# The second MLP's second product as seven products of halves, its operands streamed in steps

## What is computed

```python
def sqrelu_mlp(h, w1, w2):
    a = jax.nn.relu(h @ w1)
    return (a * a) @ w2
...
        x = x + g2 * sqrelu_mlp(hx2, w_mlp1[l], w_mlp2[l])
    return x
```

## Time and profile before

| | us |
|---|---|
| median of 3 executions | 2749.87 |
| lowest, highest | 2747.62, 2750.0 |
| the profiled execution's own time | 2747.8 |
| its span, first to last instruction | 2746.0 |
| TensorE busy in it | 2674.3 |
| the second MLP's first product (2081.2 to 2394.4) | 313.2 |
| the second MLP's second product (2394.4 to 2742.7) | 348.3 |

### The profile page before, as it was taken

The page is one execution under the profiler, slowest core; times in us unless marked ns, Lnnn a source line. Parts: engine busy times, 40 slices in busy tenths (PEclk is TensorE's granted clock), DMA queues, the critical chain, the costliest instruction groups (busy, mean ns, idle before and its releaser), DMA issues.

```text
span 2746.0 us, 41687 instructions
## 1 busy us (share of the span) xinstructions
PE 2674.3 (97%) x17264; PEld 2236.6 (81%) x17264; DVE 1582.8 (58%) x2224; ACT 1074.9 (39%) x1735; POOL 178.9 (7%) x153
## 2 busy tenths in 40 slices
PE   8999999999999999997899999999899999999999
PEld 7887878778888888886889878877787888888887
DVE  6445454476665797866525555566657656654443
ACT  6444454544434322126232443344445555521110
POOL 2222212300000000005100000000000000000000
PEclk9999999999999999999899999999999999999999
DMA  4111111213333786752323221121631333442221
GB/s 134 40 40 32 40 32 33 93 31 119 107 112 116 279 318 222 276 192 77 118 78 122 64 73 48 50 73 48 221 123 37 117 115 101 149 157 94 99 77 69
DMA packets 243676, 297.05 MB, mean 108 GB/s; under 512 B 10528, under 2 KB 190240, under 8 KB 243488
## 3 DMA queue, kind: packets, MB, share of 16 engines
q1 hardware_dynamic: 243488, 294.38, 32.0%
HBM read 238.77 MB, written 55.57 MB: 107 GB/s over the span
## 4 chain that ended last, share of the span: by engine, by line
PE 73%; ACT 4%; DVE 3%; DMA 1%; issue 1%; POOL 0%; SPq 0%; ACTq 0%; DVEq 0%
PE ps L841 8%; PE ps L850 8%; PE ps L844 8%; PE ps L807 7%; PE ps L809 7%; PE ps L811 7%; PE ps L529 2%; PE ps L513 2%; PE ps L1028 2%; PE ps L516 2%; PE ps L1029 2%; PE ps L1033 2%; PE ps L599 2%; PE ps L595 2%; PE ps L597 2%; PE ps L1003 1%
## 5 line engine op out<-in xcount | busy, mean ns | idle before, releaser
L1333 ACT ACTIVATE Whi<-Wraw 128x1024 fp32r<-128x1024 f32 x164 | 171.7, 1056 | 708.0 <-PE ps L850 433.3
L1882 DVE TENSOR_TENSOR Wlo<-Wraw,Whi 128x1024 fp32r<-128x1024 f32 x152 | 189.5, 1253 | 427.3 <-ACT Whi L1333 427.1
L807 PE MATMUL ps<-Bh,Ah 128*128 128x512 f32 x896 | 350.5, 391 | 5.3 <-ACT wb L1511 3.5
L809 PE MATMUL ps<-Bh,Al 128*128 128x512 f32 x896 | 349.2, 390 | 0.0
L841 PE MATMUL ps<-a_h,Whi 128*128 128x512 f32 x1024 | 316.0, 390 | 0.7 <-DVE R L1919 0.7
L844 PE MATMUL ps<-a_h,Wlo 128*128 128x512 f32 x1024 | 315.3, 389 | 0.0
L850 PE MATMUL ps<-a_l,Whi 128*128 128x512 f32 x1024 | 252.9, 389 | 0.0
L811 PE MATMUL ps<-Bl,Ah 128*128 128x512 f32 x640 | 249.0, 389 | 0.0
L595 PE MATMUL ps<-Whi,Hh 128*128 128x256 f32 x768 | 223.5, 291 | 7.6 <-ACT Hh L1364 7.6
L599 PE MATMUL ps<-Whi,Hl 128*128 128x256 f32 x768 | 220.0, 286 | 8.0 <-DVE Hl L1912 8.0
L841 PEld LDWEIGHTS ps<-a_h,Whi 128*128 128x128 f32 x1024 | 192.2, 188 | 41.4 <-DVE R L1919 1.1
(11 more groups left out here) (346 smaller groups left out, 4950.6 us busy)
## 6 DMA issues: line engine op xcount, KB each, us to landing
pair<-in_m_w SPq DMA_DIRECT2D x64, 512.0 KB, 5.4
a_scratch<-ub SPq DMA_DIRECT2D x128, 256.0 KB, 2.0
Wraw<-in_m_w SPq DMA_DIRECT2D x64, 512.0 KB, 4.2
a_r<-a_scratch SPq DMA_DIRECT2D x64, 512.0 KB, 5.3
Wraw<-in_w_in SPq DMA_DIRECT2D x56, 512.0 KB, 4.1
n<-in_w_ada SPq DMA_DIRECT2D x32, 512.0 KB, 5.0
mraw<-in_w_ada SPq DMA_DIRECT2D x32, 512.0 KB, 5.7
R<-in_xT SPq DMA_DIRECT2D x16, 512.0 KB, 4.5
```

The costliest lines, as they stand in the source:

```text
L807: e.matmul(o, h[:, k, :], Bh[x][:, k, :], start=first and k == 0, stop=False, skip_group_check=not first)
L809: e.matmul(o, l[:, k, :], Bh[x][:, k, :], start=False, stop=False, skip_group_check=not first)
L1333: e.activation(Whi[n % 4][:], Wraw[n % 2][:], ACT.Copy).then_inc(*S("w_hi").tick(n))
L1882: e.tensor_tensor(Wlo[n % 4][:], Wraw[n % 2][:], Whi[n % 4][:].bitcast(F), ALU.subtract).then_inc(*S("w_lo", "v").tick(n))
```

## The change

The second product of the second MLP becomes seven products of halves, once over all hidden features. The hidden features are halved (even and odd tiles of 128), the output features are halved (0 to 511 and 512 to 1023), and the tokens are halved. Each of the seven products is 512 outputs by 2048 hidden features by 512 tokens. The products come in the order 1, 5, 6, 2, 7, 3, 4 (`SX`), and each is cut into 8 steps of 256 hidden features, so there are 56 steps g. A step is 4 output tiles by 2 inner tiles by 3 matmuls, 24 matmuls.

- Four of the seven feature operands are sums or differences of quarters. VectorE makes the four of a group in the first product (`feature_sums`), and SP writes seven tiles a group instead of four, to `b_scratch`. The quarters of the second MLP now lie in two sets of seven buffers `qb`, which take `R1`'s place in SBUF. So `R1` is written to `xs_scratch` ahead of the first product and read back during the first 8 of the steps loaded later (`x_load(3, ...)`).
- The weights of products 5, 6, 7 and 3 are sums or differences too. VectorE makes them per step as the operands come (`step_sum`), for 5 and 7 from two loads, for 6 and 3 from one load and what product 5 left.
- Operands have 8 places. A step is loaded into its place when the step 8 before it is done (`step_load`), split by ScalarE and VectorE (`step_split`), and used once.
- Products 1, 6, 7 and 4 go on adding in the same two PSUM tiles, 5, 2 and 3 use the other two. A product's result is added to one or two quarters of `R1` (`add_part`, 4 operations of 128x512 each), eight such parts in all, in place of 64 additions of 128x1024. The last product's final 3 steps go tile by tile.

```diff
-        a_d = nc.dram_tensor("a_scratch", [64, P, T], F, kind="Internal").ap()
+        a_d = nc.dram_tensor("a_scratch", [32, P, T], F, kind="Internal").ap()
+        b_d = nc.dram_tensor("b_scratch", [7, 16, P, 512], F, kind="Internal").ap()
...
+        qb = [[at(f"qb{p}{i}", [P, 512], F, R1A + 14336 * p + 2048 * i) for i in range(7)] for p in range(2)]
+        places = [(S_(4), S_(5), S_(8), S_(9)), (S_(6), S_(7), S_(10), S_(11)), (H_(10), H_(11), H_(2), H_(3)),
...
-        WT += [cols256(m2_w2, 256 * j, 512 * i) for i in range(8) for j in range(4)]
...
+        SX = (1, 5, 6, 2, 7, 3, 4)
+        PART = {1: [(0, 0)], 5: [(0, 1), (1, 1)], 6: [(0, 1)], 2: [(0, 0)], 7: [(1, 1)], 3: [(0, 1)], 4: [(1, 0)]}
+        WGT = {1: [(0, 0)], 5: [(1, 0), (1, 1)], 6: [(0, 0)], 2: [(0, 1)], 7: [(0, 0), (1, 0)], 3: [(0, 1)], 4: [(1, 1)]}
+        FTR = {1: 0, 3: 1, 2: 2, 5: 3, 7: 4, 6: 5, 4: 6}
+        PLACE_LAST = (1, 5, 2, 7, 7, 4, 3, 3)
...
+        def quarter_buf(u):
+            return ub[u % 3] if u < 64 else qb[u // 4 % 2][u % 4]
...
+                if j:
+                    return stream()
...
+            def stream():
+                for i, x in enumerate(SX):
+                    banks = (0, 3) if x in (1, 6, 7, 4) else (1, 2)
+                    if x in (1, 5, 2, 3):
+                        for h, b in enumerate(banks):
+                            PS[stream_bank(x, 2 * h)] = b, filled[b]
+                            empty(b, filled[b])
+                            filled[b] += 1
...
+                    elif x in (6, 7, 4):
+                        pe.wait_ge(*(part_out(SX[i - 2], 0, m) for m in range(4)))
+                    o = lambda m: psum[banks[m // 2]][:, HALF[m % 2]]
+                    cont = x in (6, 7, 4)
+                    def parts(g, m, k):
+                        wh, wl, fh, fl = (t[g % 8] for t in (wgt_h, wgt_l, ftr_h, ftr_l))
+                        ws, fs = slice(512 * k + 128 * m, 512 * k + 128 * m + 128), HALF[k]
+                        return (wh[:, ws], fh[:, fs]), (wh[:, ws], fl[:, fs]), (wl[:, ws], fh[:, fs])
+                    def ready(g, n):
+                        if n == 0:
+                            pe.wait_ge(S("a_hi").at(32 + 2 * g), S("a_hi").at(33 + 2 * g))
+                        else:
+                            pe.wait_ge(S("a_lo").at(31 + 2 * g + n))
+                    together = 5 if x == 4 else 8
+                    for g in range(8 * i, 8 * i + together):
+                        for n in range(3):
+                            ready(g, n)
+                            mk = [(m, k) for m in range(4) for k in range(2)]
+                            for m, k in sorted(mk, key=lambda t: t[1]) if n < 2 else mk:
+                                a, b = parts(g, m, k)[n]
+                                done = n == 2 and k == 1
+                                last = done and g % 8 == 7
+                                ins = e.matmul(o(m), a, b, start=not cont and g == 8 * i and n == 0 and k == 0, stop=last,
+                                               skip_group_check=cont)
...
+                    if together < 8:
+                        for m in range(4):
+                            for g in range(8 * i + together, 8 * i + 8):
...
+            def feature_out(q, i):
+                v = 64 + 7 * (q - 16) + i
+                if v >= 67:
+                    sp.wait_ge(S("a_out", v % 3).at(v - 3))
+                e.dma_start(b_d[i, q - 16], qb[q % 2][3 if i == 4 else 4 if i == 3 else i][:]).then_inc(
+                    *S("a_out", v % 3).tick(v, 16))
+            def sums_out(q):
+                for n in range(4):
+                    sp.wait_ge(S("t_sum").at(4 * q + n))
+                    feature_out(q, 3 + n)
+            def step_load(g):
+                x, kk, p = SX[g // 8], g % 8, g % 8
+                if g >= 8:
+                    sp.wait_ge(stream_full(g - 8))
+                else:
+                    sp.wait_ge(product_full(STEP[PLACE_LAST[g], 31]))
+                    if g == 7:
+                        sp.wait_ge(S("c_scaled").at(127))
+                if g >= 4:
+                    sp.wait_ge(S("a_hi").at(33 + 2 * (g - 4)))
...
+                for n, (mh, kh) in enumerate(WGT[x]):
+                    if n:
+                        if g == 8 or g == 9:
+                            sp.wait_ge(S("a_part_hi").at(STEP[3, 30]), S("a_part_lo").at(STEP[3, 30]))
+                        else:
+                            sp.wait_ge(S("a_sum").at(2 * NS + (g - 2 if kk >= 2 else g - 18)))
+                    e.dma_start(two((other[g % 2] if n else wgt_r[p])), rows[kh][:, 2 * kk:2 * kk + 2, 512 * mh:512 * mh + 512]
+                                ).then_inc(*S("a_raw", g % 4).tick(32 + g, 16))
+                sp.wait_ge(f_out(16 + 2 * kk, FTR[x]), f_out(17 + 2 * kk, FTR[x]))
+                e.dma_start(two(ftr_r[p]), b_d[FTR[x], 2 * kk:2 * kk + 2].rearrange("q p c -> p q c")).then_inc(
+                    *S("a_raw", g % 4).tick(32 + g, 16))
+            def stream_loads():
+                last = 2 * NS
+                quarter_out(last - 3)
+                step_load(3)
+                step_load(4)
+                quarter_out(last - 2)
+                step_load(5)
+                step_load(6)
+                sums_out(31)
+                for g in range(7, 56):
+                    if 8 <= g < 16:
+                        sp.wait_ge(f_out(31, 6), f_out(31, 5), f_out(31, 4))
+                        x_load(3, g - 8, xs_d[g - 8])
+                    step_load(g)
+                    if g in (42, 50):
+                        result_out(2 if g == 42 else 7)
+                result_out(3)
+                result_out(4)
...
+                for m in range(8 * j):
+                    sp.wait_ge(out_at((PROJ[j], m), m // 7))
+                    e.dma_start(xs_d[m], R1[:, m, :]).then_inc(*S("xs_out").tick(1, 16))
                 for s in range(NS * j, NS * j + NS):
                     x, q = SEQ[s]
                     if x == 4 and q % 16 < 14:
                         pair_load(q + 2)
                     if s % NS >= 3:
+                        if SEQ[s - 3][0] == 2 and SEQ[s - 3][1] > 16:
+                            sums_out(SEQ[s - 3][1] - 1)
                         quarter_out(s - 3)
+                    if j:
+                        if s - NS in (107, 108, 111):
+                            step_load((107, 108, 111).index(s - NS))
+                        continue
...
+                if j:
+                    return stream_loads()
...
-                if u >= 3:
+                if q >= 18:
+                    dve.wait_ge(f_out(q - 2, (0, 1, 2, 4)[n]), S("t_sum").at(4 * (q - 2) + 3))
+                elif q >= 16:
+                    dve.wait_ge(S("xs_out").at(1), S("lo", "v").at(b_lo(1, 3, 3)))
+                elif u >= 3:
...
+            def feature_sums(q):
+                b11, b22, b21, b12, t1, t2_, t4 = (t[:] for t in qb[q % 2])
+                dve.wait_ge(S("c_sq").at(4 * q + 3))
+                if q >= 18:
+                    dve.wait_ge(f_out(q - 2, 3), f_out(q - 2, 5), f_out(q - 2, 6))
+                e.tensor_tensor(t1, b12, b11, ALU.subtract).then_inc(*S("t_sum").tick(4 * q))
+                dve.wait_ge(S("t_sum").at(4 * q))
+                e.tensor_tensor(b12, b22, b12, ALU.subtract).then_inc(*S("t_sum").tick(4 * q + 1))
+                e.tensor_tensor(t2_, b22, t1, ALU.subtract).then_inc(*S("t_sum").tick(4 * q + 2))
+                dve.wait_ge(S("t_sum").at(4 * q + 2))
+                e.tensor_tensor(t4, b21, t2_, ALU.subtract).then_inc(*S("t_sum").tick(4 * q + 3))
+            def step_sum(g):
...
+                dve.wait_ge(S("a_raw", g % 4).at(32 + g))
+                if x == 5:
+                    if g == 8:
+                        dve.wait_ge(product_full(2 * NS - 1), S("a_part_lo").at(2 * NS - 1))
+                    i = e.tensor_tensor(wgt_s[kk][:], wgt_r[p][:], other[g % 2][:], ALU.add)
+                elif x == 6:
+                    dve.wait_ge(S("a_hi").at(33 + 2 * (g - 8)), S("a_lo").at(33 + 2 * (g - 8)))
+                    i = e.tensor_tensor(wgt_s[kk][:], wgt_s[kk][:], wgt_r[p][:], ALU.subtract)
+                elif x == 7:
+                    i = e.tensor_tensor(wgt_r[p][:], wgt_r[p][:], other[g % 2][:], ALU.subtract)
+                else:
+                    dve.wait_ge(S("a_sum").at(2 * NS + 16 + kk))
+                    i = e.tensor_tensor(wgt_r[p][:], wgt_r[p][:], wgt_s[kk][:], ALU.subtract)
+                i.then_inc(*S("a_sum").tick(2 * NS + g))
+            def step_split(g):
+                p, x, kk = g % 8, SX[g // 8], g % 8
+                dve.wait_ge(S("a_hi").at(32 + 2 * g))
+                e.tensor_tensor(ftr_l[p][:], ftr_r[p][:], ftr_h[p][:].bitcast(F), ALU.subtract).then_inc(
+                    *S("a_lo").tick(32 + 2 * g))
...
+            def add_part(x, a):
+                mh, hf = PART[x][a]
+                for m in range(4):
```

(29 more changed lines are left out.)

107 lines of the change are left out of this document (83 added, 24 removed).

## The result

The changed kernel takes **2702.94 us** (median of 4 executions, 2702.66 to 2703.14) beside 2748.74 for the kernel before (median of 4, 2747.6 to 2750.0). The ratio is 0.9833, 95% interval 0.9816 to 0.985. The forecast was 2705 in a range of 2700 to 2720.

What follows compares the result with a forecast made beforehand. TensorE, busy 97% of the span, was taken as the bound, the second product being the pure sum of its matmuls. 2747.8 - 43.5 - 0.4 = 2703.9 us, put at 2705 towards the three executions' median; range 2700 to 2720.

Steps and rivals of the forecast that it cites:

- The sum on TensorE: Second product: 1536 matmuls removed, 1344 added at 226.7 ns each, so 43.5 us less and a stage of 304.7 us.
- The boundary: Before the first product's last quarter: TensorE's 1.03 us wait for ScalarE's copy shortens as ScalarE is free sooner, -0.4 us.
- The tail: Kernel end: half a tile's addition and one 256 KB store landing in 2.0 us, as before; 0, bounds -0.5 and +0.5.
- Saving `R1`: Before the second stage: 8 stores of 512 KB, 7 under the projection, the last landing before the first quarter is due; 0.
- The operands of the stream: Second stage's loads: 74 MB, 244 GB/s average, peak 385 in product 5, covered by loading 7 steps ahead; cost 0.
- 27 us stay: Product 5's prefetch: of a 38 us lead, landing up to 7.4 and sum with low parts 3.7 go, 27 remain.
- Rival A: Second stage: operands late at times from slower landing; with two thirds of the lead lost, some 10 us, 2715; chance 0.08.
- VectorE and ScalarE in the stream: Second stage: VectorE works 201 us and ScalarE 119 of 304.7, costing 0 while the cover holds.
- The first product: Four added sums, 2.8 us a group, 44 us in all, hidden by about 4 us of cover and VectorE's waits; 0.
- Rival B: First product: VectorE's sums come out, about 1 us each period without the cover, 16 us in all, 2721; chance 0.05.
- The clock behind a wait: After a 1.86 us TensorE wait the clock fell to 0.50 for some 2.7 us; another 1.4 us lost each time.
- The chances: Forecast with small terms (2700 to 2711) 0.78; range 2700 to 2720 a little over 0.8; faster by over 0.2% 0.94.

Runs made afterwards that it cites:

- e7_mmorder: Changed kernel with all three kinds of matmul of a stream step going tile by tile in one order: 2700.3 us.
- e1_lead4: Changed kernel with a step's loads waiting for the step 4 before it instead of 8: 2705.06 us.
- e2_lead3: Changed kernel with a step's loads waiting for the step 3 before it instead of 8: 2745.24 us.
- the moved sums: Changed kernel plus four or eight repeated subtractions a group, all sums three steps later, their stores behind the pair load: 2710.92 us with four, 2735.01 with eight.
- e9_actswap: Changed kernel with ScalarE's copy of product 6's tile ahead of the norm's inverse root in both MLPs: 2700.92 us, ratio 0.9829.
- e5_nosums: Changed kernel with the four feature sums per group written over 8 columns instead of 512: 2703.55 us.
- e10_more2: Changed kernel plus two more subtractions of 128x512 per group in the first product: 2700.61 us.

## Why the prediction was right, and where it was not

**The sum on TensorE, -43.5 us: right.** 1344 matmuls took 304.7 us at the pace of 226.7 ns, and e7_mmorder shows that the order has no part in it. Of the two paces that were weighed, the trace's gives 43.5; that of the Trainium skill (TensorE: Matmul & The Clock Gate, Part 1), 215.7 ns, gives an estimate of 41.4. 43.5 was measured.

**The boundary, -0.4: right**, measured -0.3. **The tail, 0 within 0.5: right**, measured 0.0. **Saving `R1`, 0: right**, with nothing late at the start of the stage.

**The operands of the stream, cost 0: right, but the sizes that led there were not.** "27 us stay" was 10. The 27 also left out the 6 us by which the prediction itself let the loads fall behind. Three terms were off. The full share of the DMA engines, taken as 365 GB/s from 339 at 0.93, is 389, which favours the kernel: at 365 a step's 2.10 MB would take 5.75 us against TensorE's 5.44, and the lead would have shrunk. The landing, taken as 7.4 us, is longer when the engines are full (9.8 us for the reads of x). And a step was missing from the prediction: SP's stores of the last group's sums, in which it stands for 10 us just ahead of the loads that start the peak. The stores were counted, but only in front of the pair load. How near the limit is, e1_lead4 and e2_lead3 tell: the one takes four steps of lead away and pays 0.8, the other takes five and pays 41.9. Rival A was a lead lost to loads and priced at 10 us. Its mechanism is there, ScalarE waiting for loads and TensorE for ScalarE and VectorE, but with the lead really gone it costs 42.
The Trainium skill (HBM Reference, Specifications) has about 425 GB/s for one core alone and 358 as its share when both of a pair stream. This trace has 389 with one core at work, between the two.

**VectorE and ScalarE in the stream**, predicted 201 and 119 us: 188 and 113, the additions 0.74 us each instead of 0.79, with some of the early splits done ahead of the stage. Right in what mattered. In the first product VectorE works 240.7 us, where near 249 was predicted.

**The first product, cost 0 (bounds -1 and +44): right in the number, wrong in the reason.** The step that failed is "about 4 us of cover, and within the same period VectorE waits 1.80 and 1.30 us for a product and for a load, so the delay is paid back before the next one". Every wait of VectorE was read as slack, and the load as something that comes by itself. But the pair load is issued when VectorE has freed the buffer, so a later VectorE makes a later load, and only what the loop has left counts: 1.35 us in the changed kernel. The four sums fit because the loop with them is still shorter than TensorE's 19.04 us. The prediction never compared the two, so that its 0 came true was luck: in the kernel before, VectorE is idle 3.5 to 3.9 us in this stretch in most groups, and into that the 2.8 us had to fit. Rival B had the right form, a loss once in each period, at a wrong price: 1 us a group, where work beyond the spare is paid in full. Its sum doesn't give that 1 us either: 2.8 less 1.8 and 1.3 is below 0.

**The clock behind a wait**, "another 1.4 us lost each time": not each time. It held for the wait of rows 9 in most traces, but not for each wait of that length (see the last section).

**The chances.** The prediction's own terms give its range 2700 to 2720 about 0.9, not "a little over 0.8".

**Where the total was off**: 2705 against 2702.94. The sum made against the profiled execution of before was 2703.9, and the changed kernel's profiled execution took 2702.8. The 1.1 between them is the 1.2 that came out ahead of the first product. The other 1.1, an allowance for the median of the kernel before, was not borne out.

**Not tried:** the same scheme in the first MLP, where the DMA engines carry other work; and the moved sums together with e9_actswap's exchange.

## What to carry to other kernels

When TensorE is the bound and its stage is a pure sum, cost the change by the count of matmuls and the pace in the trace, and spend the rest of the effort on the cover of everything taken as 0. Cover is not the idle share of an engine: look for the loop (buffer freed, load issued, landed, worked on, buffer freed) and compare its length with the period of the bound. And find out how far a prefetch is from the cliff by making it shorter: here a lead halved cost 0.8 us, and with one step less 42.

## What the runs showed of the hardware that was not expected

- The DMA engines moved 389 GB/s for 39 us at a share of 1.04, in loads of 512 KB, in packets of 2 KB from two tensors and of 4 KB from `xs_scratch`. While they were full (2416 to 2450 us) a tile of x took 9.8 us in the median to land and the first weight load of a step 10.5, against 4.0 for such a load over the whole stream.
- The same wait of TensorE, 1.85 to 1.88 us for the same copy, stands near the start of the first product in 13 of the traces. In 11 of them the granted clock is 0.57 to 0.60 over the next 4 us, in two (e5_nosums and e10_more2) it stays at 1.00, and 1.6 us are saved. So a difference of this size between two single executions tells nothing of a change; what decides between the two cases is not shown. The windows of these 4 us in the changed kernel, then in e5_nosums, which started 17 matmuls in them instead of 11.

```profile
2096.33:2100.33 4.00, 4.00 (x11) 3.13 (x12) 4.00 (x7) 3.44 (x6) 0.00 (x0) 0.57 0.01 4
```

```profile
2098.77:2102.77 4.00, 4.00 (x17) 3.29 (x18) 4.00 (x7) 3.92 (x7) 0.00 (x0) 1.00 0.01 4
```

- The first MLP has such a wait too, 1.68 us, and the clock stays at 1.00 behind it in all 13. In e2_lead3's stream ten waits of TensorE last 1.7 to 4.5 us: over the 4 us behind three of them (2.28, 3.28 and 4.43 us) the clock is 0.50 to 0.62, behind the other seven, one of 2.56 us among them, it is 1.00.
